# Strassen's scheme for 24 of 32 row tiles of an MLP's second matrix

## What is computed

```python
DEPTH_2 = 2
D_FF = 4 * D_MODEL            # 4096
for l in range(DEPTH_2):
    ...
    mix = jnp.concatenate([o_nsa, o_fox], axis=-1) @ w_out[l]
    x = x + _rms_norm_2(mix, g_post_mix[l])
    h = _rms_norm_2(x, g_pre_mlp[l])
    y = jnp.square(jax.nn.relu(h @ w_up[l])) @ w_down[l]
    x = x + _rms_norm_2(y, g_post_mlp[l])
```

## Time and profile before

| | |
|---|---|
| median of 3 runs | 1729.27 us (1727.81 to 1729.74) |
| the profiled execution | 1735.44 us, of which 1733.6 us span |
| PE busy | 97% of the span, 8699 matmuls |
| DVE / ACT / POOL busy | 47% / 35% / 30% |
| DMA | 79 GB/s in the mean |
| chain that ended last | PE 80%, DVE 12% |
| granted TensorE clock | 0.985 of full speed |

### The profile page before, as it was taken

One profiled execution on the slowest core, in us unless ns is written; L12 is line 12 of the kernel. 1 busy time (PEld: TensorE's weight loads), 2 busy tenths in 40 slices (PEclk: granted clock), 3 DMA queues, 4 the chain that ended last, 5 costly groups with the idle time before them and its releaser, 6 DMA issues.

```text
span 1733.6 us, 22856 instructions
## 1 busy us (share of the span) xinstructions
PE 1684.4 (97%) x8699; PEld 1269.3 (73%) x8699; DVE 823.5 (47%) x1581; ACT 599.1 (35%) x1210; POOL 518.9 (30%) x594
## 2 busy tenths in 40 slices
PE   7988999999999999999999999999999999999998
PEld 4555457488876678888888888887667888888886
DVE  7999666345337754232323264434774423232324
ACT  3233342242336644322122234233664422222222
POOL 1010001231105654615050623010564461505050
PEclk9999999998999999999999999899999999999999
DMA  6314230135220004332333224422000433232321
GB/s 189 71 25 92 67 110 1 28 111 175 67 87 12 2 1 118 113 96 87 97 98 97 86 56 128 136 62 98 2 2 1 122 110 97 93 90 97 97 85 49
DMA packets 181949, 136.74 MB, mean 79 GB/s; under 512 B 33719, under 2 KB 151218, under 8 KB 181842
## 3 DMA queue, kind: packets, MB, share of 16 engines
q1 hardware_dynamic: 175548, 128.06, 25.0%
q10 hardware_dynamic: 6294, 7.22, 1.9%
HBM read 131.00 MB, written 2.10 MB: 77 GB/s over the span
## 4 chain that ended last, share of the span: by engine, by line
PE 80%; DVE 12%; issue 2%; DMA 2%; POOL 2%; ACT 1%; ACTq 0%; DVEq 0%; POOLq 0%; SPq 0%
PE ps L420 19%; PE ps L419 19%; PE ps L421 19%; PE ps L1855 4%; PE ps L1871 3%; PE ps L1886 3%; PE ps L1055 3%; PE ps L1743 2%; DMA WR<-in_cmp_w_v 1%; PE ps L963 1%; DVE X L558 1%; PE ps L1044 1%; DMA WR<-in_w_up 1%; DVE BIG L1278 1%; PE ps L461 1%
## 5 line engine op out<-in xcount | busy, mean ns | idle before, releaser
L409 DVE TENSOR_TENSOR WR_R<-WR,WH_MLP 128x1024 fp32r<-128x1024 f32 x128 | 159.4, 1245 | 489.6 <-ACT WH_MLP L403 489.6
L421 PE MATMUL ps<-HT_R,WR_R 128*128 128x512 f32 (+1 forms) x832 | 313.8, 377 | 0.0
L403 ACT ACTIVATE WH_MLP<-WR 128x1024 fp32r<-128x1024 f32 x128 | 136.0, 1062 | 502.1 <-PE ps L421 496.9
L2393 POOL TENSOR_TENSOR BIG<-BIG 128x512 f32<-128x512 f32 x64 | 100.3, 1568 | 380.3 <-ACT BIG L2097 380.3
L420 PE MATMUL ps<-HL_MLP,WH_MLP 128*128 128x512 f32 (+1 forms) x576 | 213.8, 371 | 0.0
L419 PE MATMUL ps<-HT_R,WH_MLP 128*128 128x512 f32 (+1 forms) x576 | 213.2, 370 | 0.0
L420 PE MATMUL ps<-WR_R,uT_hi 128*128 128x512 f32 x512 | 203.3, 397 | 0.0
L421 PE MATMUL ps<-WH_MLP,uT_lo 128*128 128x512 f32 x512 | 202.1, 395 | 0.0
L419 PE MATMUL ps<-WH_MLP,uT_hi 128*128 128x512 f32 x512 | 200.1, 391 | 0.0
L421 PEld LDWEIGHTS ps<-HT_R,WR_R 128*128 128x128 f32 x832 | 157.3, 189 | 31.5
L1978 ACT ACTIVATE BIG<-ps 64x512 f32<-64x512 f32 (+3 forms) x124 | 71.8, 580 | 177.2 <-PE ps L421 163.1
(11 more groups left out here) (354 smaller groups left out, 2873.1 us busy)
## 6 DMA issues: line engine op xcount, KB each, us to landing
WR<-in_w_up SPq DMA_DIRECT2D x64, 512.0 KB, 4.1
WR<-in_w_down SPq DMA_DIRECT2D x64, 512.0 KB, 3.7
WR<-in_w_in SPq DMA_DIRECT2D x36, 512.0 KB, 5.3
WR<-in_w_out SPq DMA_DIRECT2D x6, 2048.0 KB, 7.9
...
```

Of the source, the lines that this page charges most:

```text
L403: nc.scalar.activation(hi, whole, ACT.Copy).then_inc(sem.w_hi, 1)
L409: nc.vector.tensor_tensor(lo, whole, hi.bitcast(F32), ALU.subtract).then_inc(sem.w_lo, 1)
L421: return nc.tensor.matmul(out_, w[1], x[0], start=False, stop=stop)
L2393: pool_link(nc.gpsimd.tensor_tensor(r, r, r, ALU.mult))
```

## The change

**What is computed.** For the row tiles 0 to 23 of w_down, two neighbouring row tiles make a pair (12 pairs). The pair's u is a 2x2 block matrix: A11 and A12 are the first 256 tokens of the two tiles, A21 and A22 the other 256. w_down's two row tiles by 512 columns (256 from each half of the outputs) make B. Strassen's scheme in its form with 15 additions gives A times B with 7 products of blocks in place of 8. The sums of blocks of u are S1 to S4 (each 128x256), those of the weights T1 to T4. The seven products are collected in Z over all pairs, and joined into Y once, at the end. A "step" is one pair with one half of B's columns (a "sweep"): 7 products x 2 token tiles x 3 matmuls of 256 columns, 42 in all; before, the same work was 24 matmuls of 512 columns. There are 24 steps per layer, four in a block d: steps 4d and 4d+1 (sweep 0 of pairs 2d and 2d+1), one up, steps 4d+2 and 4d+3 (sweep 1), three ups. The tiles 24 to 31 are done as before.

**Who does what.** ACT: relu (`unit_done`), the square (POOL did it before), the high parts of u and of its sums (`pair_hi`, `pair_hi_sums`), the high parts of the weights (`up_hi`, `step_hi`). POOL: S1 to S4 (`pair_sums`), T1 to T4 (`step_sums`), the low parts of u and its sums (`pair_lo`, 1792 columns for a pair). DVE: the low parts of the weights (`step_lo`, `step_lo_sums`, `up_lo`) and the collection of the products from PSUM (`collect`). PE waits at the first matmul of a step for the low parts of the pair (`u_pool`) and of the step's weights (`w_lo`).

**Besides.** One of the eight products with w_out (token tile 2, first half of the outputs) is begun earlier: five of its eight parts, 15 matmuls, stand among the last units of attention (`OUT_EARLY`), behind the turns of the probabilities (L1871 before) and ahead of the products with the values (L1886). Two semaphores of the first block are joined into one. `add_outputs` for the first half of the outputs now stands on DVE behind the sixth of the eight low parts of the last down weights.

The diff, cut to its core:

```diff
+PRODUCTS = ((A11, B11), (A12, B21), (S4, B22), (A22, T4), (S1, T1), (S2, T2), (S3, T3))
...
+        def step_hi(act, l, n):
+            u, i = by_name[f"st{n}_{l}"], n % 2
+            act.wait_ge(wring[u.slot], u.landed)
+            set_free(act, l, n)
+            nc.scalar.activation(H11[i][:], WR[:, u.slot, 0:256], ACT.Copy)
+            nc.scalar.activation(H2[i][:], WR[:, u.slot, 512:1024], ACT.Copy).then_inc(sem.w_hi, 1)
+            act.wait_ge(sem.t_sum, NSTEP * l + n + 1)
+            nc.scalar.activation(WH_MLP[2 * i + 1][:], T_ALL[i], ACT.Copy).then_inc(sem.w_hi, 1)
+        def step_sums(pool, l, n):
+            u, t = by_name[f"st{n}_{l}"], T_ALL[n % 2]
+            pool.wait_ge(wring[u.slot], u.landed)
+            set_free(pool, l, n)
+            b = WR[:, u.slot, :].rearrange("p (b c) -> p b c", c=256)
+            pool_link(nc.gpsimd.tensor_tensor(t[:, 0:512].rearrange("p (b c) -> p b c", c=256), b[:, 1::2, :], b[:, 0:2, :], ALU.subtract))
+            pool_link(nc.gpsimd.tensor_tensor(t[:, 512:768], b[:, 3, :], t[:, 0:256], ALU.subtract))
+            nc.gpsimd.tensor_tensor(t[:, 768:1024], b[:, 2, :], t[:, 512:768], ALU.subtract).then_inc(sem.t_sum, 1)
+        def step_lo(dve, l, n):
...
+            dve.wait_ge(sem.t_sum, NSTEP * l + n + 1)
+            dve.wait_ge(sem.w_hi, NSPLIT * l + step_number(n) + 1)
+            nc.vector.tensor_tensor(WR_R[:, u.slot, 0:256], WR[:, u.slot, 0:256], H11[i][:].bitcast(F32), ALU.subtract)
+            nc.vector.tensor_tensor(WR_R[:, u.slot, 512:1024], WR[:, u.slot, 512:1024], H2[i][:].bitcast(F32), ALU.subtract)\
+                .then_inc(sem.w_lo, 1)
...
+            def strassen_step(d, sweep, i):
+                n, p = 4 * d + 2 * sweep + i, 2 * d + i
+                pe.wait_ge(sem.u_pool, N_POOL * l + 2 * p + 2)
+                pe.wait_ge(sem.w_lo, NSPLIT * l + step_number(n) + 2)
+                for q, (left, right) in enumerate(PRODUCTS):
+                    if i == 0:
+                        product_bank_free(d, sweep, q)
+                    w = step_right(l, n, right)
+                    for t in range(2):
+                        c = 256 * left + P * t
+                        x = [v[:, c:c + P] for v in (U_HI[p % 3], U_LO[p % 3])]
+                        out_ = ps[product_bank(d, q)][:, 256 * t:256 * t + 256]
+                        nc.tensor.matmul(out_, x[0], w[0], start=(i == 0 and t == 0), stop=False, skip_group_check=True)
+                        nc.tensor.matmul(out_, x[0], w[1], start=False, stop=False, skip_group_check=True)
+                        last = nc.tensor.matmul(out_, x[1], w[0], start=False, stop=(i == 1), skip_group_check=True)
+                    last.then_inc(sem.prod, 1)
...
+            whole_up(4)
+            for d in range(NST):
+                strassen_step(d, 0, 0)
+                strassen_step(d, 0, 1)
+                whole_up(4 * d + 5)
+                strassen_step(d, 1, 0)
+                strassen_step(d, 1, 1)
+                for f in range(4 * d + 6, 4 * d + 9):
+                    whole_up(f)
```

The order on ACT in a block d > 0, where b is 4d+3 and c is 4d+4:

```diff
+                else:
+                    unit_done(b - 1)
+                    up_hi(act, l, c)
+                    step_hi(act, l, 4 * d)
+                unit_done(b)
+                pair_hi(2 * d + 1)
+                up_hi(act, l, c + 1)
+                step_hi(act, l, 4 * d + 1)
+                pair_hi_sums(2 * d + 1)
+                unit_done(c)
```

On DVE, the first part of a block, and the low parts of the last down weights:

```diff
+            for d in range(NST):
+                if d:
+                    collect(d - 1, 1, range(7))
+                up_lo(dve, l, 4 * d + 4)
+                step_lo(dve, l, 4 * d)
+                step_lo_sums(dve, l, 4 * d)
+                up_lo(dve, l, 4 * d + 5)
+                step_lo(dve, l, 4 * d + 1)
+                step_lo_sums(dve, l, 4 * d + 1)
+                collect(d, 0, (0, 1))
...
+            for i in range(8):
+                down_lo(dve, l, i)
+                if i == 5:
+                    add_outputs(dve, l, 0, range(T))
```

On POOL:

```diff
+            def pair_sums(p):
+                part = lambda i: U_ALL[p % 3][:, 256 * i:256 * i + 256]
+                pool.wait_ge(sem.u_act, N_ACT * l + 5 * p + 3)
+                pool_link(nc.gpsimd.tensor_tensor(part(S1), A21_[:, p % 2, :], part(A22), ALU.add))
+                pool_link(nc.gpsimd.tensor_tensor(part(S2), part(S1), part(A11), ALU.subtract))
+                nc.gpsimd.tensor_tensor(part(S3), part(A11), A21_[:, p % 2, :], ALU.subtract)
+                nc.gpsimd.tensor_tensor(part(S4), part(A12), part(S2), ALU.subtract).then_inc(sem.u_pool, 1)
+            def pair_lo(p):
+                pool.wait_ge(sem.u_pool, N_POOL * l + 2 * p + 1)
+                for n, cols_ in enumerate((slice(0, 768), slice(768, 1792))):
+                    pool.wait_ge(sem.u_act, N_ACT * l + 5 * p + 4 + n)
+                    last = nc.gpsimd.tensor_tensor(U_LO[p % 3][:, cols_], U_ALL[p % 3][:, cols_], U_HI[p % 3][:, cols_].bitcast(F32),
+                                                   ALU.subtract)
+                last.then_inc(sem.u_pool, 1)
+            for d in range(NST):
+                if d == 0:
+                    pair_sums(0)
+                    step_sums(pool, l, 0)
+                    pair_lo(0)
+                else:
+                    step_sums(pool, l, 4 * d)
+                pair_sums(2 * d + 1)
+                step_sums(pool, l, 4 * d + 1)
+                pair_lo(2 * d + 1)
+                step_sums(pool, l, 4 * d + 2)
+                step_sums(pool, l, 4 * d + 3)
+                if d + 1 < NST:
+                    pair_sums(2 * d + 2)
+                    pair_lo(2 * d + 2)
```

More of the change, by code:

```diff
@@ L1889, in values, with out_product @@
                 last.then_inc(sem.o_ps, 1)
+            def out_product(e, k_from, k_to):
+                t, half = MIX_ORDER[e]
+                for k in range(k_from, k_to):
+                    pe.wait_ge(sem.mixT_lo, KD * l + k + 1)
+                    w = [v_.rearrange("p (k c) -> p k c", c=512)[:, k % 2, :] for v_ in split(pe, l, J_OUT + 4 * half + k // 2)]
+                    x = [v_[:, k, P * t:P * t + P] for v_ in (HT_R, HL_MIX[1])]
+                    last = product(ps[mid_bank(t, half)][:], x, w, k == 0, k == KD - 1)
+                return last
+            OUT_EARLY = {NU2 + 1: (0, 3), NU2 + 2: (3, 5)}
             for u in range(NU2 + 4):
@@ new lines, in two_pe, with down_right @@
+            for f in range(4 * NST + 5, NF):
+                whole_up(f)
+            def down_right(i, half):
+                pe.wait_ge(sem.w_lo, NSPLIT * l + J_DOWN + 4 * half + i // 2 + 1)
+                _, hi, lo, _ = down_parts(l, 4 * half + i // 2)
+                return [v[:, 512 * (i % 2):512 * (i % 2) + 512] for v in (hi, lo)]
+            pe.wait_ge(sem.z_sum, z_count(l, NST - 1, 1, 6))
+            for i in range(FG):
+                pe.wait_ge(sem.u_pool, N_POOL * l + 2 * NPAIR + i + 1)
+                w = down_right(i, 0)
+                for t in range(T):
+                    x = [v[:, i, P * t:P * t + P] for v in (uT_hi, uT_lo)]
+                    last = product(ps[in_bank(t, 0)][:], x, w, i == 0, i == FG - 1)
+                if i % 2:
+                    last.then_inc(sem.down, 1)
@@ new lines, in two_pe @@
+            pe.wait_ge(sem.u_act, N_ACT * (l + 1))
+            for t in range(T):
+                for i in range(FG):
+                    w = down_right(i, 1)
+                    x = [v[:, i, P * t:P * t + P] for v in (uT_hi, uT_lo)]
+                    last = product(ps[in_bank(t, 1)][:], x, w, i == 0, i == FG - 1)
+                last.then_inc(sem.down, 1)
+                if l + 1 < DEPTH and t >= 2:
+                    norm_transpose(pe, v + 2, t - 2)
+        BANKS = (0, 1, 2, 3, 5, 6, 7, 4)
@@ new lines, in collect @@
+            def collect(d, sweep, products):
+                for q in products:
+                    dve.wait_ge(sem.prod, step_done(l, 4 * d + 2 * sweep) + q + 1)
+                    src = ps[product_bank(d, q)][:].rearrange("p (t c) -> p t c", t=2)
+                    z = Z[q][:, :, 256 * sweep:256 * sweep + 256]
+                    if d == 0:
+                        nc.vector.tensor_copy(z, src).then_inc(sem.z_sum, 1)
+                    else:
+                        dve.wait_ge(sem.z_sum, z_count(l, d - 1, sweep, q))
+                        nc.vector.tensor_tensor(z, src, z, ALU.add).then_inc(sem.z_sum, 1)
@@ new lines, in two_dve @@
+            collect(NST - 1, 1, range(7))
+            up_lo(dve, l, F_PLAIN + 4)
+            dve.wait_ge(sem.z_sum, z_count(l, NST - 1, 1, 6))
+            plus = lambda i, j: nc.vector.tensor_tensor(Z[i], Z[i], Z[j], ALU.add)
+            plus(1, 0)
+            plus(2, 4)
+            dve_link(plus(5, 0))
+            plus(2, 5)
+            dve_link(plus(6, 5))
+            up_lo(dve, l, F_PLAIN + 5)
+            dve_link(plus(3, 6))
+            dve_link(plus(4, 6))
+            for f in range(F_PLAIN + 6, NF):
+                up_lo(dve, l, f)
```

(1 more changed line is left out.)

366 lines of the change are left out of this document (240 added, 126 removed).

## The result

The changed kernel takes 1795.53 us in the median (1783.26 to 1801.33), the kernel before 1729.51 beside it: a ratio of 1.036, 95% interval 1.030 to 1.043. The likeliest forecast, 1775, was 20 us short of it; the range and the direction held. It is the longest of the four: the shortest, 1783.26 us, had a mean granted clock of 0.980 where this one had 0.970, and (0.980 - 0.970) of the span is the 18 us between them. All ratios are over fast executions, and only one execution of all was slow, 3261.96 us in experiment 8.

A forecast was written before the change was run, and what follows sets the result against it. PE, 97% busy, was taken to bound the kernel by matmul count times start distance. PE's gain, ten pauses, first blocks, `add_outputs` and clock: -30.2 + 42 + 21.4 + 2.8 + 10 = +46 on 1729.3, 1775 us; range 1736 to 1806.

The forecast's parts named there:

- PE's gain: MLP steps on PE: 42 narrow matmuls take 4.92 us instead of 5.55, over 48 steps 30.2 us less.
- The ten pauses: Before step 4d+1 in blocks 1 to 5: PE stands 4.2 us each, 42 us; 1.6 each without contention.
- 0.85 us lost for each us shared: POOL and DVE two-input instructions: they hold each other up, losing some 0.85 us per us run together.
- The first blocks: Each layer's first block: PE stands 2.3 us before step 0 and 8.4 before step 1, 21.4 us together.
- The clock: PE's clock falls to 1.2 GHz behind the long pauses and a few of the ten: 10 us, from 0 to 35.
- one of its own signs of being wrong: PE's clock at its pauses: the prediction would be wrong if the clock fell at none or all of them.
- Rival D: All 14 PE pauses: the clock falls at each and comes back late, 14 x 3.4 = 48 us, 1813; chance 0.12.
- Joining the products: On DVE after the paired tiles: 7 instructions of 1.23 us hidden behind six ups, free.
- `add_outputs`: DVE, ahead of the last two low parts of the down weights: PE waits 1.4 us a layer, 2.8 us.
- The early output product: End of attention: moves 3.5 us of work but fills no gap, worth 0 with 0.5 either way.
- Collecting the products: DVE's `collect`, one operand from PSUM: 14 x 0.69 us a block, behind the steps, free.
- Rival C: Chain behind the pair is covered and PE's gain comes through: 1710 us, 1700 to 1728; chance 0.10.

The follow-up runs named there:

- experiment 8: Changed kernel plus a second 1024-column DVE instruction on the low part of up 4d+5's weights, blocks 1 to 5: 1808.08 us, ratio 1.0449 to the kernel before.
- experiment 3: Changed kernel with the low and high parts of up 4d+5's weights moved behind those of step 4d+1: 1777.62 us, ratio 1.0244 to the kernel before.
- experiment 9: As experiment 3, with DVE's low parts of step 4d+1 cut to 16 columns for d from 1 to 5 (output wrong): 1749.29 us, ratio 1.0117 to before.
- experiment 6: As experiment 5, with DVE taking both pairs' low parts from POOL in each layer's first block: 1714.04 us, ratio 0.9896 to the kernel before.
- experiment 5: Changed kernel with step 4d+1's weights' sums ahead of the pair's in blocks 1 to 5, plus experiment 4's edit: 1725.90 us, ratio 0.9962 to before.
- experiment 4: Changed kernel with low parts of ups 29 to 31 between the joining additions and `add_outputs` after all eight last low parts: 1782.26 us, ratio 1.0262 to before.
- experiment 7: As experiment 6, but the product with w_out whole and in its old place: 1711.46 us, ratio 0.9891 to the kernel before.

## Why the prediction was right, and where it was not

**The account.** The prediction had the mechanism right: PE waits ahead of every second step of sweep 0, for a chain on POOL that DVE's work lengthens. Between the spans: less matmul work -25.9, pauses at the steps +58.2, two waits for the low part of up 29 +6.7, for the last down weights +1.9, clock in the MLPs +23.9. That is 64.8 of 65.7 us. Outside the MLPs the clock cost 5.0 us less in the second layer's attention and 4.2 us more in the first 640 us than in the execution of before, which the change explains in neither place; with these 1.7 us stay without a row. Against the forecast's +46 the terms differ by 4.3 for PE, -5.2 for the pauses at the steps, 6.7 for the up, -0.9 for the last down weights and 13.9 for the clock.

**PE's gain** was put at 30.2 us and is 48 x (5.55 - 5.01) = 25.9. The direction of the step is right, its size 14% off: 84 matmuls take 10.02 us, 0.1193 each, where the half ups of the earlier trace rows have 0.1172. Why a step's matmuls lie 2 ns further apart was not tried and stays open.

**The ten pauses**: forecast 4.2 us each, measured 3.89, 38.9 us in all for 42. The mechanism, DVE and POOL one at a time, is shown by experiments 3, 8 and 9: 1.30 nearly without contention (the prediction's lower bound was 1.6), 3.89 with it, and about 1 us for each DVE instruction of 1.23 us put in or taken out. Two of its details were off. The prediction has 0.85 us lost for each us shared; the runs show whole turns: who comes second ends about its own length after the other's instruction has ended. And the last to be ready is not POOL's 1024 columns but DVE's L548, which waits for them. The Trainium skill, "SBUF — State Buffer", section "SBUF: two separate sides", has it so: a GpSimd instruction and a VectorE one with two SBUF inputs take turns at a shared port pair, each for its whole length. By that rule DVE's 16 columns should end behind POOL's instruction; the trace of experiment 9 agrees, they end at 1458.78 and POOL's 768 columns at 1458.76.

**The first blocks**: forecast 10.7 us a layer (2.3 and 8.4), measured 2.29 + 7.32 = 9.6. The prediction's own terms for the second of these add up to 13.5, not 13.3 us, and 14.8 - 10.5 for the ten pauses is 4.3, not 4.2; neither slip changes the reading. Experiment 6 against experiment 5 shows that another order and another engine for the low parts take 10 of the remaining 16 us away.

**The clock** is the mis-sized term: 10 us forecast, 23.9 measured, the largest part of the 20 us by which the forecast of 1775 fell short. The prediction let it fall behind the long pauses and a few of the ten; it fell at all ten. (A fall at all of the pauses was one of its own signs of being wrong, and only the two of 2.3 us were missing.) The 1.7 us a fall costs here is inside its 1.5 to 3.4 and below the 2.5 that it took, so the number of falls was too low and not their price. The long pauses cost 4.9 us for 5 forecast, the ten 16.2 for 5, and 2.9 fell behind the wait at up 29, which it did not have. Besides, PE's gain came out 4.3 us smaller and the pauses 5.2 shorter than forecast; that these two cancel is luck. Rival D had the pauses right (12 of 14) and the price wrong, 3.4 us each where a fall behind 3.89 us costs 1.7: 48 forecast. The Trainium skill, "TensorE: Matmul & The Clock Gate", section "HAM oscillation", the rule that stood behind D, has the clock fall at every such wait; by that rule all ten pauses lose time; the trace of the changed kernel agrees, ten of ten, and experiment 3, at 2.90 us, shows six of ten. The wait of 3.36 us ahead of up 29 brought it down in one layer of the changed kernel and not in the other.

**Joining the products** was costed at nothing, "behind six ups": this step failed. The ups cover the seven additions together, but the queue holds five of them in a row ahead of a low part that PE needs, and each takes 1.9 us beside POOL. It cost 3.4 us a layer, and experiment 4 took it away. **`add_outputs`**: 1.4 us a layer forecast, 0.9 measured. **The early output product**: nothing, as forecast; experiment 7 shows no difference that can be told. **Collecting the products** costs POOL nothing, as forecast. One of its operands is in PSUM, and that is where it differs from the DVE instructions above; no run changes this alone. In the changed kernel POOL's two low parts of the even pair take 4.22 us, 1.84 + 2.39 by the prediction's line for POOL alone, while seven of these run on DVE.

```profile
1509.72 4.22 POOL L2708 TENSOR_TENSOR U_LO<-BIG,U_HI 128x768 fp32r<-128x768 f32 x2
...
1509.96 5.00 DVE L2567 TENSOR_TENSOR BIG<-ps,BIG 128x512 f32<-128x512 f32 x7 [0.92 <-PE ps L2117]
```

**Rival C**, that the gain comes through, was the wrong reading of this order of work, but it is what the scheme gives in another: experiment 6 keeps every matmul of the change and is 1.0% faster than the kernel before. The prediction's 0.2% for what can be told apart was too fine: the kernel before itself ran from 1721 to 1740 us.
